# Attention in a two-block transformer: third and fourth maximum and the diagonal follow one another on VectorE; the products of a head's first maximum run one head ahead on TensorE

## The chip, the cores and the metric

The kernel runs on one core of one Trainium2 chip. The metric is the device time of an execution in microseconds (us); lower is better. The five engines of a core (TensorE or PE, VectorE or DVE, ScalarE or ACT, GpSimd or POOL, SyncE or SP) each work through their own queue in order and wait on each other through semaphores. "PEld" in the profile is TensorE's loading of weights, which overlaps its matmuls.

## What is computed

The reference is two transformer blocks on 512 tokens of width 1024. The part that matters here is the attention of the first block: 8 query heads over 2 key and value heads, 512 latent queries against 768 keys (256 of a context, 512 latent).

```python
def gqa_block(q, k, v):
    B, Q = q.shape[:2]
    qg = q.reshape(B, Q, ATTN_KV_HEADS, GQA_GROUP, HEAD_DIM)
    s = jnp.einsum('bqkgd,btkd->bkgqt', qg, k, preferred_element_type=jnp.float32) * ATTN_SCALE
    p = jax.nn.softmax(s, axis=-1).astype(v.dtype)
    o = jnp.einsum('bkgqt,btkd->bqkgd', p, v)
    return o.reshape(B, Q, ATTN_WIDTH)
```

The softmax subtracts each query's maximum over the 768 keys. After the attention the heads are multiplied by `w_out`. Beside it the kernel still has to compute 24 "modulation rows", dot products of a conditioning vector with 128 rows of `w_mod` each, which nothing needs before the attention is over.

## The kernel before

One program for each engine, written out by hand; what stands in the code is the order in which an engine runs. Products are made of rounded high parts and low remainders (`q_high`, `q_low`, `Kst`, `K2`), so a head's scores take two matmuls for each tile.

The attention is one loop over the 8 heads, with these steps for head h:

- **First pass, for the maxima (TensorE, L814 `row_max(h, qt)`, qt 0 to 3).** 128 queries on the partitions, 768 keys along the free dimension: two matmuls of 512 and two of 256 columns, into banks 0 and 1 (even qt) or 2 and 3 (odd qt). VectorE's `att_max(h, qt)` (L1958) reduces the 768 columns to one maximum for each query. A bank pair is free again once the maximum before the last was taken (`pe.wait_ge(a_mx, u - 1)`).
- **Diagonal and row (VectorE, then TensorE).** `att_diagonal(h)` spreads the four columns of maxima over four diagonal blocks `Dg`; `shift_row(h)` (matmul L839) multiplies them by ones, which gives the negative maxima as a row over the 512 queries in bank 4. ScalarE (`shift_high`, L1290) and VectorE (`shift_low`, L1978) write it into spare partitions of `q_low`, so that the second pass subtracts it.
- **Second pass (TensorE, `scores(h, kt)`, kt 0 to 5, L850 and L851).** 128 keys on the partitions, 512 queries along the free dimension, in banks 4 and 5 by turns. `scores(h, 0)` waits for `shift_low(h)`. ScalarE takes the exponential (`exponent`, L1298) into `PA` or `PB`, and `values(h, kt)` (L863) accumulates the product with the values, and the sum of the exponentials.
- **Scaling.** ScalarE's `inverse_sum(h)` (L1307, L1308), after the second exponential of the next head; VectorE's `att_scale(h)` (L1986) and, for each pair of heads, `att_low` (L1991).
- **Queries of the next pair.** VectorE's `query_low(t, e)` (L1949, L1950) in iterations 0, 2 and 4, once ScalarE's `query_high` is there.
- **Modulation rows.** VectorE's `modulation_row` (L1930) reads one 512 KB unit that SyncE has loaded into one of the four buffers `wraw`. Each row read lets SyncE load the next unit: unit k of this row series needs k - 3 rows read; behind the 24 units come the units of `w_out`, whose first needs 21 rows read, the second 22. Between them stands the load of `crow`.

Iteration h of the loop holds the second pass of head h and the first pass of head h + 1. ScalarE's order around the last head is fixed: before `exponent(7, 4)` stands the rounding of the first unit of `w_out` (`split_hi`, L580), which waits for that unit's load.

In the words of the rows below, "head h" stands for iteration h. Iterations 1, 3 and 5 are called odd, 2, 4 and 6 even.

## Time and profile before

| | |
|---|---|
| median of 3 runs | 1503.74 us (1501.14 to 1504.5) |
| the profiled execution | 1504.83 us, span 1503.0 us |
| TensorE busy | 1420.6 us, 95% of the span |
| VectorE busy | 913.9 us, 61% |
| ScalarE busy | 540.7 us, 36% |
| the chain that ended last | TensorE 86%, VectorE 9%, ScalarE 2% |
| the loop over heads | from 266.89 us (`scores(0, 0)`) to 366.27 us (first matmul of `w_out`) |

TensorE's busy share is that of the whole program; its matmuls are pipelined, so in a stretch where TensorE waits now and then, the waits have to be read from the rows. The profiled execution took 1.1 us more than the median of the runs.

### The profile page before, as it was taken

To read this page: it belongs to the slowest core of one execution; us is meant where nothing else is said; L and a number is where in the kernel's file an instruction comes from. 1 tells how busy PE (TensorE), PEld (TensorE's weight loads), DVE (VectorE), ACT (ScalarE), POOL (GpSimd) and SP (SyncE) were. 2 spreads that over 40 slices of the span, in tenths; PEclk is the share of its full clock that TensorE was granted. 3 is DMA by queue.
4 is the path that set the end of the run, shared out by engine and by line. 5 is a ranking of instruction groups with operands and counts; after the bars stand their busy time and mean duration, and the time that the engine had idled before them with its cause. 6 is when DMAs were issued, how large, how long until landed. Compare 5 with 4: busy or idle time off the path is not lost.

```text
span 1503.0 us, 16624 instructions
## 1 busy us (share of the span) xinstructions
PE 1420.6 (95%) x6132; PEld 1103.4 (73%) x6132; DVE 913.9 (61%) x1232; ACT 540.7 (36%) x754; POOL 102.7 (7%) x117
## 2 busy tenths in 40 slices
PE   6899999999969999999999999999879999999996
PEld 4688887555738888888884487767768888888885
DVE  5744487886166666663235674888537888886222
ACT  2523353544352323222222553332343433333221
POOL 0002530000300000000110020000020000000010
PEclk9799999999989999999999999999989999999999
DMA  9222230235216666664421022120112322323211
GB/s 371 81 77 84 78 107 21 85 112 182 84 50 245 209 223 223 213 235 143 152 81 43 28 85 70 57 100 26 56 70 85 98 98 87 108 89 126 100 62 56
DMA packets 44514, 169.19 MB, mean 113 GB/s; under 512 B 5516, under 2 KB 6092, under 8 KB 43181
## 3 DMA queue, kind: packets, MB, share of 16 engines
q1 hardware_dynamic: 43052, 165.60, 31.5%
q0 software_dynamic: 1408, 2.89, 0.7%
q8 instruction: 33, 0.54, 0.1%
q14 instruction: 21, 0.16, 0.0%
HBM read 163.49 MB, written 2.10 MB: 110 GB/s over the span
## 4 chain that ended last, share of the span: by engine, by line
PE 86%; DVE 9%; ACT 2%; issue 2%; DMA 1%; SPq 0%; POOL 0%; DVEq 0%; ACTq 0%
PE PS L597 71%; PE PS L966 4%; PE PS L654 2%; DVE tb L1698 2%; DVE sink L1930 1%; PE PS L1087 1%; DVE H L1698 1%; DVE dert L1958 1%; PE PS L617 1%; PE PS L642 1%; PE PS L863 1%; DMA wraw<-w_mod_a 1%; DVE wsp L586 1%; PE PS L839 1%; PE PS L725 1%
## 5 line engine op out<-in xcount | busy, mean ns | idle before, releaser
L597 PE MATMUL PS<-H,wsp 128*128 128x512 f32 x3600 | 843.5, 395 | 26.6 <-DVE H L1698 17.7
L597 PEld LDWEIGHTS PS<-H,wsp 128*128 128x128 f32 x3600 | 681.3, 190 | 183.9 <-issue 23.4
L586 DVE TENSOR_TENSOR wsp<-wraw,wsp 128x1024 fp32r<-128x1024 f32 (+1 forms) x182 | 237.3, 1304 | 439.5 <-ACT wsp L580 439.2
L580 ACT ACTIVATE wsp<-wraw 128x1024 fp32r<-128x1024 f32 (+1 forms) x182 | 202.6, 1114 | 523.7 <-PE PS L597 522.0
L597 PE MATMUL PS<-hid,wsp 128*128 128x512 f32 x1056 | 240.0, 389 | 0.0
L597 PEld LDWEIGHTS PS<-hid,wsp 128*128 128x128 f32 x1056 | 198.2, 188 | 41.8 <-issue 0.8
L1698 DVE SCALAR_TENSOR_TENSOR cva<-PS,dert,cva 128x441 f32<-128x441 f32 (+2 forms) x176 | 122.2, 695 | 5.5
L1930 DVE CUSTOM_DVE_ANT_0 sink<-mring,crow_t,colt 128x1024 bf16<-128x1024 f32 x56 | 71.7, 1280 | 0.4
L1621 POOL COPY acc<-sqb 128x512 f32<-128x512 f32 x4 | 4.4, 1093 | 809.9 <-ACT sqb L1413 287.5
L1624 POOL TENSOR_TENSOR acc<-acc,sqb 128x512 f32<-128x512 f32 x24 | 41.2, 1717 | 202.0 <-ACT sqb L1599 82.6
L654 PE MATMUL PS<-sqb,ones 128*128 128x512 f32 (+1 forms) x64 | 34.8, 696 | 8.9 <-ACT sqb L1126 8.8
L1397 ACT ACTIVATE hid<-hv 128x512 f32 (+1 forms) x22 | 13.9, 632 | 70.3 <-DVE hv L2113 70.3
L1698 DVE SCALAR_TENSOR_TENSOR ca<-cb__144,colt,ca 128x512 f32<-128x512 f32 x40 | 33.8, 845 | 3.2 <-ACT ca L1478 2.5
L654 PEld LDWEIGHTS PS<-sqb,ones 128*128 128x128 f32 x64 | 13.8, 244 | 28.4 <-issue 17.1
L1644 POOL DMA_DIRECT2D RS<-RU x44 | 21.8, 502 | 183.2 <-ACT RU L1221 146.8
L1579 ACT ACTIVATE sl<-cva,colt 128x512 f32<-128x512 f32 x22 | 15.9, 725 | 49.9 <-DVE cva L1698 49.9
L1126 ACT ACTIVATE sqb<-X 128x512 f32<-128x512 f32 x32 | 19.9, 627 | 38.4 <-PE PS L654 23.0
L1958 DVE TENSOR_REDUCE dert<-PS 128x1 f32<-128x768 f32 x32 | 30.4, 950 | 4.1 <-PE PS L829 3.9
L1930 DVE CUSTOM_DVE_ANT_0 sink<-wraw,crow_t,colt 128x1024 bf16<-128x1024 f32 x24 | 30.7, 1278 | 0.4
L1131 ACT ACTIVATE H<-tb,dert 128x512 fp32r<-128x512 f32 x32 | 22.3, 721 | 22.9 <-DVE tb L1698 22.9
L597 PEld LDWEIGHTS PS<-Hc,wsp 128*128 128x128 f32 x240 | 30.0, 192 | 0.7
L597 PE MATMUL PS<-Hc,wsp 128*128 128x256 f32 x240 | 30.2, 283 | 0.0
(277 smaller groups left out, 1295.0 us busy)
## 6 DMA issues: line engine op xcount, KB each, us to landing
mring<-mod_c SPq DMA_DIRECT2D x56, 512.0 KB, 4.5
wraw<-w_ffn_in SPq DMA_DIRECT2D x44, 512.0 KB, 3.3
wraw<-w_up SPq DMA_DIRECT2D x44, 512.0 KB, 3.2
wraw<-w_mod_b SPq DMA_DIRECT2D x24, 512.0 KB, 3.3
wraw<-w_hy_in SPq DMA_DIRECT2D x24, 512.0 KB, 3.2
wraw<-w_w_in SPq DMA_DIRECT2D x22, 512.0 KB, 3.2
wraw<-w_ffn_out SPq DMA_DIRECT2D x16, 704.0 KB, 4.1
wraw<-w_down SPq DMA_DIRECT2D x16, 704.0 KB, 4.0
```

The costliest lines, as they stand in the source:

```text
L580: nc.scalar.activation(wsp[:, o % 2, 0, 0:n], wraw[:, g % RAW, 0:n], ACT.Copy).then_inc(w_hi, 1)
L586: nc.vector.tensor_tensor(wsp[:, o % 2, 1, 0:n], wraw[:, g % RAW, 0:n], wsp[:, o % 2, 0, 0:n].bitcast(F32), ALU.subtract).then_inc(w_lo, 1)
L597: mm = nc.tensor.matmul(psum, wsp[:, o % 2, a, wk * P:(wk + 1) * P], h[:, b, kt, :], start=first and kt == kts[0] and (a, b) == (0, 0), st ...
L654: nc.tensor.matmul(PS[:, bank, 0:n], ones[:, :], sqb[:, q % 2, 0:n], start=kt == 0, stop=kt == KT - 1).then_inc(n_acc, 1)
L966: mm = nc.tensor.matmul(PS[:, b0 + a, :], fwdt[:, a, mt, f * P:(f + 1) * P], src[:, (a // 2) * 2 + mt, c * 512:(c + 1) * 512], start=mt == ...
L1126: SC.activation(sqb[:, q % 2, 0:n], src, ACT.Square).then_inc(n_sq, 1)
L1131: SC.activation(dst, tb[:, (k * KT + kt) % 4, 0:n], ACT.Identity, bias=shift).then_inc(n_hi, 1)
L1624: PL.tensor_tensor(acc_of(k), acc_of(k), sqb[:, q % 2, 0:n], ALU.add).then_inc(n_acc, 1)
L1644: ins = pool.dma_start(moved_tile(n)[to:to + HALF, :], RU[of:of + HALF, n % 2, 0:L])
L1698: return VE.scalar_tensor_tensor(out=o, in0=a, scalar=s, in1=b, op0=op0, op1=op1)
L1930: VE.tensor_tensor_reduce(sink[:, :], unit, crow_t[:, which, :], 1.0, bias, ALU.mult, ALU.add, to).then_inc(m_rd, 1)
L1958: VE.tensor_reduce(der("mx", u), PS[:, b:b + 2, :].rearrange("p a b -> p (a b)")[:, 0:LA], mybir.AxisListType.X, ALU.max).then_inc(a_mx, 1)
```

## The change

On TensorE `row_max(h + 1, 0)` leaves its place behind `scores(h, 0)` and is issued at the end of the iteration before, behind `values(h - 1, 5)`; that of head 1 stands ahead of the loop. On VectorE `att_max(h + 1, 0)` moves in the same way, behind `shift_low`. `att_max(h + 1, 2)`, `att_max(h + 1, 3)` and `att_diagonal(h + 1)` follow one another, where a modulation row or a half of `query_low` stood between the second and third, and another between the third and fourth maximum. The pieces taken out go behind the diagonal, behind the first maximum, and to the iteration's end. ScalarE's, GpSimd's and SyncE's orders stay as they are, and no instruction is added or dropped.

```diff
--- before.py
+++ after.py
@@ -883,10 +883,9 @@
                     inner_values(t)
             shift_row(0)
             gn_variance(3)
+            row_max(1, 0)
             for h in range(8):
                 scores(h, 0)
-                if h < 7:
-                    row_max(h + 1, 0)
                 scores(h, 1)
                 if h < 7:
                     row_max(h + 1, 1)
@@ -899,6 +898,8 @@
                     shift_row(h + 1)
                 values(h, 4)
                 values(h, 5)
+                if h < 6:
+                    row_max(h + 2, 0)
 
 
             pe.wait_ge(a_mx, 32)
@@ -2034,9 +2035,8 @@
             gn_low(1)
             shift_low(0)
             dve.wait_ge(crow_on, 1)
+            att_max(1, 0)
             for h in range(8):
-                if h < 7:
-                    att_max(h + 1, 0)
                 if h == 0:
                     gn_scale(2)
                     gn_gate(3)
@@ -2044,34 +2044,32 @@
                     att_scale(h - 1)
                 if h < 7:
                     att_max(h + 1, 1)
+                if h == 0:
+                    gn_scale(3)
+                    gn_low(2)
+                elif h < 7:
+                    modulation_row(next(mod_next))
+                if h < 7:
+                    att_max(h + 1, 2)
+                    att_max(h + 1, 3)
+                    att_diagonal(h + 1)
                 if h % 2 == 0 and h < 6:
                     query_low(h // 2 + 1, 0)
                 elif h < 7:
                     modulation_row(next(mod_next))
                 if h < 7:
-                    att_max(h + 1, 2)
-                if h == 0:
-                    gn_scale(3)
-                    gn_low(2)
-                elif h % 2 == 0 and h < 6:
+                    shift_low(h + 1)
+                if h < 6:
+                    att_max(h + 2, 0)
+                if h % 2 == 0 and h < 6:
                     query_low(h // 2 + 1, 1)
                 elif h < 7:
                     modulation_row(next(mod_next))
-                if h < 7:
-                    att_max(h + 1, 3)
-                    att_diagonal(h + 1)
                 if h == 0:
-                    query_low(1, 1)
+                    gn_low(3)
                 elif h % 2 == 0:
                     att_low(h // 2 - 1)
-                if h % 2 and h < 7:
-                    modulation_row(next(mod_next))
                 if h < 7:
-                    shift_low(h + 1)
-                    modulation_row(next(mod_next))
-                if h == 0:
-                    gn_low(3)
-                if h % 2 == 0 and h < 6:
                     modulation_row(next(mod_next))
             for m in mod_next:
                 modulation_row(m)
```

On TensorE, around the end of iteration 0 and the start of iteration 1 (L839 is the row of maxima, L863 the values, L828 and L829 the products for a maximum, L850 and L851 the scores), the order changes like this:

```order
 L863 MATMUL PS<-PA,V 128x512 x2
-L850 MATMUL PS<-H,Kst 128x512
-L851 MATMUL PS<-H,K_96 128x512
-L828 MATMUL PS<-Kst,QS_93 128x512
-L829 MATMUL PS<-K_96,QS_93 128x512
-L828 MATMUL PS<-Kst,QS_93 128x256
-L829 MATMUL PS<-K_96,QS_93 128x256
+L828 MATMUL PS<-Kst,QS_93 128x512
+L829 MATMUL PS<-K_96,QS_93 128x512
+L828 MATMUL PS<-Kst,QS_93 128x256
+L829 MATMUL PS<-K_96,QS_93 128x256
+L850 MATMUL PS<-H,Kst 128x512
```

Rows with "-" are the order of before, rows with "+" that of the change. The four products for the maximum now stand between the last values and the first scores.

On VectorE, before, from the shift of head 4 (iteration 3's end) to the diagonal of head 5 (iteration 4), where L1978 is `shift_low`, L1930 a modulation row with its accumulator read, L1958 a maximum, L1986 `att_scale`, L1949 and L1950 a half of `query_low`:

```order
267 L1978 TENSOR_TENSOR H<-PS,H 32x512
268 L1930 ISA sink,dert<-wraw,crow_t,colt 128x1024
270 L1958 TENSOR_REDUCE dert<-PS 128x1
271 L1986 TENSOR_TENSOR R<-PS,R 64x512
272 L1958 TENSOR_REDUCE dert<-PS 128x1
273 L1949 CAST QS_93<-QA 64x512
274 L1950 TENSOR_TENSOR QS_93<-QA,QS_93 64x512
275 L1958 TENSOR_REDUCE dert<-PS 128x1
276 L1949 CAST QS_93<-QA 64x512
277 L1950 TENSOR_TENSOR QS_93<-QA,QS_93 64x512
278 L1958 TENSOR_REDUCE dert<-PS 128x1
279 L1698 SCALAR_TENSOR_TENSOR Dg<-ident,dert 128x512
```

And the same stretch of the change (its lines have numbers one higher):

```order
259 L1979 TENSOR_TENSOR H<-PS,H 32x512
260 L1959 TENSOR_REDUCE dert<-PS 128x1
261 L1931 ISA sink,dert<-wraw,crow_t,colt 128x1024
263 L1931 ISA sink,dert<-wraw,crow_t,colt 128x1024
265 L1987 TENSOR_TENSOR R<-PS,R 64x512
266 L1959 TENSOR_REDUCE dert<-PS 128x1
267 L1931 ISA sink,dert<-wraw,crow_t,colt 128x1024
269 L1959 TENSOR_REDUCE dert<-PS 128x1 x2
270 L1699 SCALAR_TENSOR_TENSOR Dg<-ident,dert 128x512
```

The first maximum now stands right behind the shift, three modulation rows stand before the third maximum instead of one, and both halves of `query_low` have gone behind the diagonal. (The accumulator read behind each modulation row is left out of both listings.)

On VectorE, before, from the last diagonal to the first low part of `w_out` (L1991 is `att_low`, L586 the low part of a unit):

```order
310 L1698 SCALAR_TENSOR_TENSOR Dg<-ident,dert 128x512
311 L1991 TENSOR_TENSOR H<-R,H 128x512
312 L1978 TENSOR_TENSOR QS_93<-PS,QS_93 32x512
313 L1930 ISA sink,dert<-wraw,crow_t,colt 128x1024
315 L1986 TENSOR_TENSOR R<-PS,R 64x512
316 L1930 ISA sink,dert<-wraw,crow_t,colt 128x1024
318 L1930 ISA sink,dert<-wraw,crow_t,colt 128x1024
320 L1930 ISA sink,dert<-wraw,crow_t,colt 128x1024
322 L586 TENSOR_TENSOR wsp<-wraw,wsp 128x1024 x2
```

And the same stretch of the change:

```order
299 L1699 SCALAR_TENSOR_TENSOR Dg<-ident,dert 128x512
300 L1931 ISA sink,dert<-wraw,crow_t,colt 128x1024
302 L1979 TENSOR_TENSOR QS_93<-PS,QS_93 32x512
303 L1931 ISA sink,dert<-wraw,crow_t,colt 128x1024
305 L1992 TENSOR_TENSOR H<-R,H 128x512
306 L1931 ISA sink,dert<-wraw,crow_t,colt 128x1024
308 L1987 TENSOR_TENSOR R<-PS,R 64x512
309 L1931 ISA sink,dert<-wraw,crow_t,colt 128x1024
311 L1931 ISA sink,dert<-wraw,crow_t,colt 128x1024
313 L1931 ISA sink,dert<-wraw,crow_t,colt 128x1024
315 L586 TENSOR_TENSOR wsp<-wraw,wsp 128x1024 x2
```

Behind the last diagonal and ahead of `att_scale(6)` there were one modulation row and `att_low`; now there are three rows and `att_low`. The 21st row is in both orders the last one ahead of `att_scale(6)`.

## Rows read from the trace of the kernel before

**Rows 1.** Timeline of TensorE: start us, duration us, engine, line, tiles, idle before and releaser

```profile
276.79 1.13 PE L839 MATMUL PS<-Dg,ones 128*128 128x512 f32 x2 [0.65 <-DVE Dg L1698]
...
292.89 0.39 PE L828 MATMUL PS<-Kst,QS 128*128 128x512 f32 x1
...
302.77 1.12 PE L839 MATMUL PS<-Dg,ones 128*128 128x512 f32 x2 [1.20 <-DVE Dg L1698]
...
305.30 0.55 PE L850 MATMUL PS<-QS,Kst 128*128 128x512 f32 x1
...
315.67 1.12 PE L839 MATMUL PS<-Dg,ones 128*128 128x512 f32 x2 [1.04 <-DVE Dg L1698]
...
354.71 1.13 PE L839 MATMUL PS<-Dg,ones 128*128 128x512 f32 x2 [1.31 <-DVE Dg L1698]
```

**Rows 2.** Timeline of VectorE in an even iteration, head 2

```profile
293.78 0.96 DVE L1958 TENSOR_REDUCE dert<-PS 128x1 f32<-128x768 f32 x1 [0.22 <-PE PS L829]
...
299.88 0.42 DVE L1949 CAST H<-QA 64x512 fp32r<-64x512 f32 x1
...
301.03 0.96 DVE L1958 TENSOR_REDUCE dert<-PS 128x1 f32<-128x768 f32 x1
302.03 0.69 DVE L1698 SCALAR_TENSOR_TENSOR Dg<-ident,dert 128x512 f32<-128x512 f32 x1
...
304.56 0.68 DVE L1978 TENSOR_TENSOR QS<-PS,QS 32x512 fp32r<-32x512 f32 x1 [1.24 <-ACT QS L1290]
```

**Rows 3.** Timeline of VectorE in an odd iteration, head 3

```profile
305.27 1.28 DVE L1930 CUSTOM_DVE_ANT_0 sink<-wraw,crow_t,colt 128x1024 bf16<-128x1024 f32 x1
...
306.60 1.28 DVE L1930 CUSTOM_DVE_ANT_0 sink<-wraw,crow_t,colt 128x1024 bf16<-128x1024 f32 x1
...
309.20 0.68 DVE L1986 TENSOR_TENSOR R<-PS,R 64x512 f32<-64x512 f32 x1 [0.32 <-ACT R L1308]
309.81 0.94 DVE L1958 TENSOR_REDUCE dert<-PS 128x1 f32<-128x768 f32 x1
310.67 1.27 DVE L1930 CUSTOM_DVE_ANT_0 sink<-wraw,crow_t,colt 128x1024 bf16<-128x1024 f32 x1
...
311.87 0.94 DVE L1958 TENSOR_REDUCE dert<-PS 128x1 f32<-128x768 f32 x1
```

**Rows 4.** Timeline of VectorE in an even iteration, head 6

```profile
347.98 0.69 DVE L1986 TENSOR_TENSOR R<-PS,R 64x512 f32<-64x512 f32 x1 [1.41 <-ACT R L1308]
348.70 0.96 DVE L1958 TENSOR_REDUCE dert<-PS 128x1 f32<-128x768 f32 x1
349.69 1.29 DVE L1930 CUSTOM_DVE_ANT_0 sink<-wraw,crow_t,colt 128x1024 bf16<-128x1024 f32 x1
```

**Rows 5.** Timeline of all engines around head 7 and the start of `w_out`

```profile
358.53 9.68 SPq L466 DMA_DIRECT2D wraw<-w_w_out  x6
...
362.14 1.05 ACT L580 ACTIVATE wsp<-wraw 128x1024 fp32r<-128x1024 f32 x1
...
363.09 0.58 ACT L1298 ACTIVATE PB<-PS 128x512 f32<-128x512 f32 x1
...
364.10 1.98 PE L863 MATMUL PS<-PB,V 128*128 128x512 f32 x4
...
366.27 2.96 PE L597 MATMUL PS<-H,wsp 128*128 128x512 f32 x12 [0.20 <-DVE wsp L586]
```

**Rows 6.** DMA issues from 353.3 to 355 us, and from 358 to 359 us: KB each, us to landing

```profile
wraw<-w_mod_b SPq DMA_DIRECT2D x1, 512.0 KB, 3.4
...
wraw<-w_w_out SPq DMA_DIRECT2D x1, 512.0 KB, 3.4
```

**Rows 7.** Stretches of 1 us: busy us of PE, PEld, DVE, ACT, POOL, then PE clock, DMA share, GB/s

```profile
355.00:356.00 1.00, 1.00 (x3) 0.39 (x3) 0.26 (x1) 0.13 (x1) 0.00 (x0) 1.00 0.99 385
...
380.00:381.00 1.00, 1.00 (x4) 0.81 (x3) 1.00 (x1) 0.78 (x2) 0.62 (x1) 0.50 0.81 246
```

**Rows 8.** Timeline of TensorE ahead of the third unit of `w_out`

```profile
379.20 21.16 PE L597 MATMUL PS<-H,wsp 128*128 128x512 f32 x85 [1.81 <-DVE wsp L586]
```

## The prediction, made before the changed kernel ran

> **What bounds the kernel now.** I read the busy table first: TensorE works 95% of the span, so only its waits can be won back. Then TensorE's timeline through the loop over heads. Before every row of maxima (L839) TensorE stands still until VectorE's diagonal is done: 0.65 us in head 0, later 1.04, 1.20 and 1.31 us [rows 1]. From the first of these rows in the loop, at 276.79 us, to the last, at 354.71 us, there are six whole periods: 77.92 us, 12.99 us each [rows 1]. Within a period TensorE has about 11.8 us of work (302.77 to 315.67 us is 12.90 us, less the wait of 1.04 us [rows 1]). The most that the loop can give is therefore 6 x 1.2 = 7 us, 0.5% of the kernel.
>
> Then VectorE's timeline, since it is what TensorE waits for. I measure from start to start, because that is what adds up. VectorE reads its products in an order that makes it wait first for ScalarE (0.32 us ahead of `att_scale` in head 3 [rows 3], 1.41 us in head 6 [rows 4]) and then run without a pause to the diagonal. So the diagonal is late because of what stands between `att_scale` and it, and the change takes pieces out of just that stretch. The question is what VectorE waits for once they are gone.
>
> **The clockwork.** I put time 0 at the start of a row of maxima (L839) and call it T. Each fixed distance comes from one pair of rows:
>
> - the diagonal starts at T - 0.74 (302.03 against 302.77 us) [rows 1, 2];
> - `shift_low` starts at T + 1.79 (304.56 us) [rows 2], and the next head's first scores at T + 2.53 (305.30 us) [rows 1];
> - on VectorE, start to start: `att_scale` to maximum 0.61, maximum to modulation row 0.86, modulation row to maximum 1.20, modulation row to modulation row 1.33 (all [rows 3]); in even heads, where `att_scale` works on the other half of the partitions, `att_scale` to maximum 0.72 and maximum to modulation row 0.99 [rows 4]; half a `query_low` to the next instruction 1.15 (299.88 to 301.03 us), maximum to diagonal 1.00 [rows 2]. For maximum to maximum, of which the trace has no unwaited pair, I take 0.86 as to a modulation row; 1.00 would be its upper bound. For `att_low` I take 0.61, that of `att_scale`.
>
> **The change part by part.**
>
> *TensorE.* The four products of the first maximum move ahead of `scores(h + 1, 0)`. Their place is T + 2.53, but the values ahead of them still stream: the first scores took 0.55 instead of 0.39 us there [rows 1], so I add 0.16 and let them start at T + 2.69. VectorE took the maximum 0.89 us after such products began (292.89 to 293.78 us) [rows 1, 2]. So the first maximum starts at T + 3.58 and no sooner. TensorE's own work stays what it was. The wait for `shift_low`, which the values alone just covered, is now covered with 0.7 us to spare, and is worth nothing.
>
> *VectorE.* After `shift_low` (done at T + 2.5) stands the first maximum, and VectorE idles until T + 3.58. That is a new wait of about 1.1 us in each head, and behind it stands everything that leads to the next diagonal. From there, in an even head: maximum 0.99, two modulation rows 1.33 each, `att_scale` 0.72, maximum 0.99, modulation row 1.20, maximum 0.86, maximum to diagonal 1.00. The sum is 8.42, the diagonal stands at T + 12.00 and the next row of maxima at T + 12.74. In an odd head: maximum 0.99, half a `query_low` 1.15, `att_low` 0.61, modulation row 1.20, `att_scale` 0.61, maximum 0.86, modulation row 1.20, maximum 0.86, and 1.00 to the diagonal. That is 8.48, and T + 12.80. ScalarE's part of `att_scale` was there at T + 6.43 in head 3 (309.20 us) [rows 1, 3] and comes a little later now, about T + 6.6; VectorE gets to `att_scale` at about T + 7.2, so that old wait is gone. TensorE waits a little before the products of the fourth maximum, whose banks come free when the second is read, but finishes the last scores at about T + 12.6, still ahead of the row.
>
> Six periods, three of each kind, make 76.6 us against 77.9: **the loop gives 1.3 us**. Head 0 I cost at 0.1 us gained: there VectorE still stands before `gn_low(2)` until ScalarE has its copy ready behind the fourth exponential, which covers all that was pulled forward. If that cover were gone, head 0 would give at most its wait of 0.65 us [rows 1].
>
> *The tail.* Here a price stands that is easy to miss. Of the 24 modulation rows fewer are read early: one instead of two in head 0, four instead of three in head 6. The 21st row, which lets SyncE load the first unit of `w_out`, was read right behind the last `shift_low`; that load was issued at 358.53 us, T + 3.82 [rows 1, 5]. Now behind `shift_low` (T + 2.51) stand row 20, `att_low` and row 21: 1.20 + 0.61 later, so the load goes out at T + 5.65. Row 20 in turn releases the last unit of the modulation rows and the load of `crow`, at T + 3.85; before, they went out a good 5 us ahead of `w_out`. So three transfers of 512 KB are in flight together. Alone such a unit lands 3.4 us after its issue [rows 6], and at the full rate of 385 GB/s [rows 7] each further one needs 512 KB / 385 GB/s = 1.36 us. They land at T + 7.25, 8.6 and 9.95. Bounds for the first unit of `w_out`: T + 9.05 if nothing gets in its way, T + 9.95 if all queue up; I take the later one, since the rate in the row is that of full DMA engines (0.99 busy).
>
> Who waits for it: ScalarE's `split_hi`, and behind it on ScalarE `exponent(7, 4)` and `exponent(7, 5)`, and for them TensorE's last two value products and with them `w_out`. Before, ScalarE was free for it at 362.14 us (T + 7.43) and found it landed. It took 0.95 us to the next exponential, and TensorE went on at 364.10 us without a pause, T + 9.39 [rows 5]. Now: 9.95 + 0.95 + 0.65 for the exponential = T + 11.5. So TensorE idles about 2.1 us, and `w_out` starts 2.1 us later than it would, at T + 13.6 instead of T + 11.56 (366.27 us [rows 1, 5]). With the early landing it is 1.2 us. **The tail takes 2.1 us.** Nothing after that changes its order.
>
> *Sum.* -1.3 - 0.1 + 2.1 = +0.7 us. Against the profiled execution's own 1504.83 us this is 1505.5; its median of runs lies 1.1 us lower, which gives **1504.4 us**. A measurement of this kernel can hardly tell less than 0.2%, 3.0 us, from no change.
>
> *A rule against the trace.* In the rows a modulation row starts 0.86 us after a maximum that lasts 0.94 us [rows 3], so VectorE's instructions overlap a little when none waits for another. The Trainium skill (VectorE: DVE Perf Modes, "The DRAIN you can't avoid") says that the next instruction does not start until the pipeline has emptied, and that chaining without semaphores does not help. By the trace the stretch to the diagonal takes 8.4 to 8.5 us; by that rule it would take more, as in the third rival below.
>
> **The rivals.**
>
> 1. *The tail costs more: the clock falls.* TensorE waited 1.81 us before 379.20 us [rows 8], and from 380 us its granted clock was 0.50, which is 1.2 of its 2.4 GHz [rows 7]; by the stretches beside it that lasted some 3.3 us, which costs 1.7 us of work. Not each such wait does this: of nine waits of 1.3 to 2.5 us in the trace I found a fall after three. A wait of 2.1 us in the tail is of that kind. Time: 1504.4 + 1.7 = 1506.1 us.
> 2. *The tail costs less.* The first unit of `w_out` lands by T + 9.05, 0.9 us sooner: 1503.5 us. For it: of the 3.4 us that a lone unit takes only 1.36 are movement at full rate, and the two transfers ahead of it have been under way for 1.8 and 1.4 us when it starts.
> 3. *Slower, from VectorE.* With two maxima in a row on other banks, and with semaphores between most pieces, each instruction starts only when the one before has ended. With full lengths (maximum 0.99, modulation row 1.36, `att_scale` and `att_low` 0.72) the stretches become 8.8 and 9.3 us, the periods 13.1 and 13.6, and six of them 80.1 us: 2.2 us slower instead of 1.3 faster. Time: 1504.4 + 3.5 = 1507.9 us, slower. That is 0.065 us for each of some nine instructions in six periods; from about 0.045 us each it decides, since 2.4 us more than the forecast is where slower begins. Against it: the same pairs overlap in the trace of before.
> 4. *Faster: TensorE becomes the bound.* If the first maximum came with no wait and VectorE were ready early in each head, the periods would be TensorE's 11.8 us: 7.1 us less, with the tail still 2.1 us more. Time: 1503.74 - 5.0 = 1498.7 us. Against it: VectorE can't start the first maximum before T + 3.58 and has 8.4 us of work from there to the diagonal.
>
> **How the numbers follow.** Forecast 0.45, rival 1 0.22, rival 2 0.13, rival 3 0.11, rival 4 0.09. The forecast, rival 1 and rival 2 all lie within 3.0 us of 1503.74, together 0.80; slower is rival 3, 0.11; faster is rival 4, 0.09. The range leaves out rival 4 and most of rival 3. It reaches down below rival 2 by the scatter of the runs, to 1502.0 us, and up past rival 1 to 1506.9 us.
>
> **What the changed kernel's profile would show.** Rows of maxima in the loop 12.7 to 12.8 us apart, with TensorE's wait for the diagonal down to 0.1 to 0.4 us; a wait of VectorE of about 1 us for the product of each first maximum, and none for ScalarE ahead of `att_scale`; a short wait of TensorE for the second maximum; the first load of `w_out` 5.6 us after the last row of maxima, ScalarE's first `split_hi` of `w_out` waiting for a DMA, and TensorE standing still for 1 to 2 us ahead of its last values. I am wrong if that load is not waited for (then it is faster by 1.4 us), if the periods stay at 13 us, or if they fall under 12.3.

## The result and the profile after

| | before | changed |
|---|---|---|
| median, first comparison | 1502.99 us (1499.59 to 1504.85, 20 runs) | 1505.97 us (1503.13 to 1508.52, 20 runs) |
| ratio, first comparison | | 1.0026, 95% interval [1.0019, 1.0033] |
| median, second comparison (`e11_change_timed`) | 1502.73 us (15 runs) | 1505.19 us (11 runs) |
| ratio, second comparison | | 1.0015, 95% interval [1.0006, 1.0024] |
| profiled execution | 1504.83 us, span 1503.0 us | 1505.25 us, span 1503.5 us |

The change makes the kernel slower: by 3.9 us (2.9 to 5.0) in the first comparison and 2.3 us (0.9 to 3.6) in the second. The mean of the two is 3.1 us. The busy table has hardly moved (page of the changed kernel; busy us, share of the span, instructions):

```profile
span 1503.5 us, 16624 instructions
PE 1419.8 (94%) x6132; PEld 1100.9 (73%) x6132; DVE 914.9 (61%) x1232; ACT 540.1 (36%) x754; POOL 102.1 (7%) x117
```

So the difference lies in waits, and in the clock. The spans of two single executions don't show it, since the program ahead of the loop and behind it scatters: in the thirteen traces of this study head 0's row of maxima starts anywhere from 260.3 to 264.5 us, and from the third unit of `w_out` to the end it takes 1121 to 1124 us. The second scatter goes with TensorE's clock: in six of the traces (before, changed, `e1`, `e2`, `e3`, `e9`) the granted clock falls to 0.50 just behind the third unit's wait, and the rest takes 1123.6 to 1124.3 us; in the other seven it stays at 1.00 there, and the rest takes 1121.1 to 1122.6 us. Executions of the changed kernel lie in both groups. I therefore compare stretches between fixed points: the eight rows of maxima (L839), the last head's last values (L863 behind the wait), and the start of the third unit of `w_out`, which waits 1.81 us for VectorE in each of the traces that I compare below. Each row of such numbers is one execution; of the kernel before there is one trace only.

| us | before | changed | difference |
|---|---|---|---|
| head 0: first row of maxima to second | 12.44 | 12.29 | -0.15 |
| loop: second to eighth row, six periods | 77.92 | 76.62 | -1.30 |
| eighth row to the last values | 9.39 | 12.15 | +2.76 |
| last values to the third unit of `w_out` | 15.10 | 16.38 | +1.28 |
| together | 114.85 | 117.44 | +2.59 |

TensorE's timeline of the changed kernel has these points (start, duration, idle before and what ended it). They answer to [rows 1] and [rows 8]:

```profile
274.21 1.12 PE L839 MATMUL PS<-Dg,ones 128*128 128x512 f32 x2 [1.19 <-DVE Dg L1699]
...
283.35 0.50 PE L828 MATMUL PS<-Kst,QS 128*128 128x512 f32 x1 [0.64 <-DVE dert L1959]
...
287.01 1.12 PE L839 MATMUL PS<-Dg,ones 128*128 128x512 f32 x2
...
299.76 1.12 PE L839 MATMUL PS<-Dg,ones 128*128 128x512 f32 x2 [0.16 <-DVE Dg L1699]
...
350.83 1.13 PE L839 MATMUL PS<-Dg,ones 128*128 128x512 f32 x2 [0.17 <-DVE Dg L1699]
...
362.98 3.52 PE L863 MATMUL PS<-PB,V 128*128 128x512 f32 x4 [2.58 <-ACT PB L1299]
365.51 12.04 PE L597 MATMUL PS<-H,wsp 128*128 128x512 f32 x48
...
379.36 2.14 PE L597 MATMUL PS<-H,wsp 128*128 128x512 f32 x6 [1.81 <-DVE wsp L586]
```

From the second row on, the waits for the diagonal have shrunk from 1.04 to 1.31 us to nothing or 0.17 us (in head 0 the wait has grown, from 0.65 to 1.19 us), and a new one of 0.64 us has come up inside the first pass. But the period is only 0.22 us shorter. And between the last row of maxima and the last values there is now a wait of 2.58 us where there was none.

VectorE's timeline in iteration 1 shows why the loop gives so little:

```profile
276.00 0.68 DVE L1979 TENSOR_TENSOR H<-PS,H 32x512 fp32r<-32x512 f32 x1 [0.69 <-ACT H L1291]
277.79 0.96 DVE L1959 TENSOR_REDUCE dert<-PS 128x1 f32<-128x768 f32 x1 [1.11 <-PE PS L829]
...
281.75 0.68 DVE L1987 TENSOR_TENSOR R<-PS,R 64x512 f32<-64x512 f32 x1
...
284.42 1.81 DVE L1959 TENSOR_REDUCE dert<-PS 128x1 f32<-128x768 f32 x2
286.26 0.69 DVE L1699 SCALAR_TENSOR_TENSOR Dg<-ident,dert 128x512 f32<-128x512 f32 x1
```

The first maximum (277.79 us) waits 1.11 us for its product; the old wait ahead of `att_scale` (L1987) is gone; the third and fourth maximum are one group (x2) and take 1.81 us together; the diagonal follows at once. One wait has taken the place of the other.

The tail, in a timeline of SyncE and one of ScalarE (the first start of a group of SyncE is the issue of its first load):

```profile
355.04 0.42 SPq L526 DMA_DIRECT2D crow_t<-crow  x1
356.47 3.69 SPq L466 DMA_DIRECT2D wraw<-w_w_out  x3
...
361.39 1.06 ACT L580 ACTIVATE wsp<-wraw 128x1024 fp32r<-128x1024 f32 x1 [3.00 <-DMA wraw<-w_w_out]
362.35 1.07 ACT L1299 ACTIVATE PB<-PS 128x512 f32<-128x512 f32 x2
```

In [rows 5] the load of `w_out` went out 3.82 us after the last row of maxima, and ScalarE found it landed. Now it goes out after 5.64 us, is there 4.9 us later, and ScalarE has stood still for 3.00 us in front of `split_hi`, with the two exponentials (x2, 362.35 us) behind it that TensorE needs.

Then the clock. Stretches of 1 us (busy us of PE, PEld, DVE, ACT, POOL; then the granted clock of PE, the DMA share, GB/s):

```profile
358.00:359.00 1.00, 1.00 (x5) 0.66 (x4) 0.96 (x3) 0.38 (x1) 0.00 (x0) 1.00 1.14 401
359.00:360.00 1.00, 1.00 (x4) 0.48 (x3) 0.96 (x3) 0.00 (x0) 0.00 (x0) 1.00 0.82 324
360.00:361.00 1.00, 0.40 (x2) 0.00 (x0) 1.00 (x1) 0.00 (x0) 0.00 (x0) 1.00 0.88 205
361.00:362.00 1.00, 0.00 (x0) 0.00 (x0) 0.13 (x2) 0.61 (x1) 0.00 (x0) 1.00 0.82 328
...
364.00:365.00 1.00, 1.00 (x2) 0.41 (x2) 0.61 (x1) 0.36 (x1) 0.00 (x0) 0.50 0.99 377
365.00:366.00 1.00, 1.00 (x3) 0.34 (x1) 0.62 (x1) 0.00 (x0) 0.00 (x0) 0.50 0.99 193
```

TensorE did nothing from 360.4 to 363.0 us, and behind it the granted clock was 0.50 (1.2 of 2.4 GHz), back at 1.00 from 367 us on. In the kernel before it stood at 1.00 from 363 to 369 us.

### The profile page after: what moved, and what is told of

It is laid out like the page before. It is cut to its first block, busy times and chain, and to the rows that moved or that the text cites. A ratio compares the mean times of both kernels' runs of the same rounds, so it can differ in the third digit from the quotient of the medians.

```text
span 1503.5 us, 16624 instructions
## 1 busy us (share of the span) xinstructions
PE 1419.8 (94%) x6132; PEld 1100.9 (73%) x6132; DVE 914.9 (61%) x1232; ACT 540.1 (36%) x754; POOL 102.1 (7%) x117
## 4 chain that ended last, share of the span: by engine, by line
PE 86%; DVE 9%; issue 2%; ACT 2%; DMA 1%; SPq 0%; POOL 0%; DVEq 0%; ACTq 0%
PE PS L597 71%; PE PS L967 4%; PE PS L654 2%; DVE tb L1699 2%; DVE dert L1959 1%; PE PS L863 1%; DVE sink L1931 1%; PE PS L1088 1%; DVE H L1699 1%; PE PS L617 1%; PE PS L642 1%; DMA wraw<-w_mod_a 1%; DVE wsp L586 1%; PE PS L839 1%; PE PS L725 1%
## 5 line engine op out<-in xcount | busy, mean ns | idle before, releaser
L586 DVE TENSOR_TENSOR wsp<-wraw,wsp 128x1024 fp32r<-128x1024 f32 (+1 forms) x182 | 238.0, 1308 | 440.4 <-ACT wsp L580 439.9
```

The source lines that it names most:

```text
L586: nc.vector.tensor_tensor(wsp[:, o % 2, 1, 0:n], wraw[:, g % RAW, 0:n], wsp[:, o % 2, 0, 0:n].bitcast(F32), ALU.subtract).then_inc(w_lo, 1)
```

## The experiments

All times are device medians against the kernel before on the same chip. `e1` to `e4` share one set of runs of it (1501.91 us, 21 runs), `e5` to `e8` another (1502.68 us, 29 runs). The table has the stretches of the section above.

| us | head 0 | six periods | row 8 to last values | to third unit | together, against before | ratio |
|---|---|---|---|---|---|---|
| before | 12.44 | 77.92 | 9.39 | 15.10 | 0 | |
| changed | 12.29 | 76.62 | 12.15 | 16.38 | +2.59 | 1.0026, 1.0015 |
| `e1_row_early` | 12.30 | 76.59 | 10.05 | 14.70 | -1.21 | 0.9998 [0.9988, 1.0007] |
| `e2_row_late` | 12.47 | 77.82 | 12.64 | 14.68 | +2.76 | 1.0021 [1.0011, 1.0030] |
| `e3_wait_filled` | 12.28 | 71.04 | 9.87 | 14.69 | -6.97 | 0.9952 [0.9936, 0.9968] |
| `e4_maxima_together` | 12.98 | 71.62 | 9.96 | 14.72 | -5.57 | 0.9955 [0.9941, 0.9968] |
| `e5_crow_later` | 12.28 | 76.62 | 11.63 | 16.34 | +2.02 | 1.0000 [0.9987, 1.0014] |
| `e6_split_behind` | 12.29 | 76.63 | 25.92 to the third unit | | -0.01 | 0.9994 [0.9983, 1.0005] |
| `e7_first_ahead` | 11.76 | 80.50 | 24.54 to the third unit | | +1.95 | 1.0013 [1.0001, 1.0025] |
| `e8_best` | 10.94 | 70.94 | 24.14 to the third unit | | -8.83 | 0.9936 [0.9920, 0.9951] |
| `e9_change_again` | 12.29 | 76.62 | 12.14 | 16.37 | +2.57 | |
| `e10_change_third` | 12.28 | 76.61 | 11.90 | 16.33 | +2.27 | |
| `e11_change_timed` | 12.29 | 76.63 | 13.30 | 17.56 | +4.93 | 1.0015 [1.0006, 1.0024] |

My theory: the loop gains 1.3 us and no more, because VectorE waits for the product of the first maximum; the tail loses more than that, because the 21st modulation row is read one or two instructions later and the first unit of `w_out` with it; and the clock falls on top. The rivals: the loss comes from VectorE (its instructions back to back cost more than they did apart), or from the products moved ahead on TensorE, and the tail would have been hidden.

### The tail alone: `e1_row_early` and `e2_row_late`

`e1` is the change with one more modulation row read in head 0, where VectorE waits 2.4 us for ScalarE anyway. All later rows move up by one, so the load of `w_out` goes out where it did before.

```diff
                 if h == 0:
                     gn_scale(3)
+                    modulation_row(next(mod_next))
                     gn_low(2)
```

> The change, with one modulation row more in head 0, in VectorE's wait for ScalarE's copy (2.44 us ahead of gn_low(2) in the changed kernel's profile). The 21st row is then read one place earlier and the first load of w_out goes out about 1.8 us earlier, with the load of crow well ahead of it. Theory A (the loss is the late load of w_out's first unit, with the fall of TensorE's clock behind the wait for it; the loop itself gains 1.3 us): TensorE's wait of 2.6 us ahead of its last values is gone, the granted clock stays at 1.00 there, and the kernel is 1.0 to 1.5 us faster than before, ratio 0.999 to 0.9995; from the last row of maxima to w_out 11.5 us instead of 14.7. Theory B (the loss sits in the rearranged loop or behind it, and the late load only takes up slack): the wait goes but the time stays within 1 us of the changed kernel's, ratio about 1.002.

Rows of `e1`, timelines of SyncE, ScalarE and TensorE:

```profile
354.45 7.29 SPq L466 DMA_DIRECT2D wraw<-w_w_out  x5
...
359.07 1.06 ACT L580 ACTIVATE wsp<-wraw 128x1024 fp32r<-128x1024 f32 x1 [0.91 <-DMA wraw<-w_w_out]
...
360.67 1.98 PE L863 MATMUL PS<-PB,V 128*128 128x512 f32 x4 [0.48 <-ACT PB L1299]
```

`e2` is the other half: the kernel before, with its maxima and its products where they were, and one modulation row fewer in head 0 and one more in head 6, behind `att_low(2)`. The rows between come one place later too, and the 21st is read where the change reads it.

```diff
-                elif h % 2 == 0:
+                elif h % 2 == 0 and h < 6:
                     att_low(h // 2 - 1)
...
-                if h % 2 == 0 and h < 6:
+                if h == 6:
+                    att_low(2)
+                if h in (2, 4, 6):
                     modulation_row(next(mod_next))
```

> The kernel before, with its loop untouched but for the rows: one modulation row fewer in head 0, one more in head 6, and att_low(2) between the last two, so that the 21st row is read as late after the last row of maxima as in the change. Theory A: w_out's first load goes out at about T + 5.6 and lands 4.3 to 5 us later, TensorE waits 2 to 2.6 us ahead of its last values and its clock falls to 0.50 for about 3 us in some or all executions; from the last row of maxima to w_out 13.6 to 14.7 us, and the kernel is 2 to 4 us slower than before, ratio 1.0015 to 1.0027. Theory B: no more than 0.5 us slower.

Rows of `e2`, the same timelines:

```profile
357.26 5.01 SPq L466 DMA_DIRECT2D wraw<-w_w_out  x4
...
362.67 1.06 ACT L580 ACTIVATE wsp<-wraw 128x1024 fp32r<-128x1024 f32 x1 [3.52 <-DMA wraw<-w_w_out]
...
364.27 1.98 PE L863 MATMUL PS<-PB,V 128*128 128x512 f32 x4 [3.10 <-ACT PB L1298]
```

And the stretch of 1 us in which `w_out` starts, granted clock 1.00:

```profile
365.00:366.00 1.00, 1.00 (x4) 0.38 (x2) 0.32 (x1) 0.65 (x1) 0.00 (x0) 1.00 0.70 274
```

With the load at 3.83 us behind the row (354.45 against 350.62 us), TensorE's wait falls from 2.58 to 0.48 us, the clock stays at 1.00, and the loss is gone: 0.9998. With the load at 5.63 us (357.26 us) and the maxima untouched, the kernel is slower by 3.2 us (1.7 to 4.5), about as much as with the whole change. So the late row in the tail is what turns the change into a loss. In the trace of `e2` the clock did not fall, though TensorE stood still for 3.10 us.

### What the two moves are worth in the loop: `e3`, `e4`, `e7`

`e3` is `e1` with VectorE's wait filled: the piece that stands behind the first maximum goes ahead of it.

```diff
-                if h < 6:
-                    att_max(h + 2, 0)
                 if h % 2 == 0 and h < 6:
                     query_low(h // 2 + 1, 1)
                 elif h < 7:
                     modulation_row(next(mod_next))
+                if h < 6:
+                    att_max(h + 2, 0)
```

> e1 with the piece that stood behind the first maximum (a modulation row, in even heads the second half of query_low) put ahead of it, into VectorE's wait of 1.1 us for the product. Theory A (VectorE's chain from T + 3.58 to the diagonal sets the period, and the wait ahead of it is what the move of the first maximum costs): each period falls from 12.77 to 11.8 or 11.9 us, where TensorE's own work ends it, six of them gain 5 to 6 us over e1, and the kernel is 6 to 7 us faster than before, ratio 0.9955 to 0.996. Theory B (the period is already near what TensorE and ScalarE allow): under 2 us faster than e1.

`e4` keeps the third and fourth maximum and the diagonal together, with `e1`'s early row, but both engines take the first maximum where the kernel before did.

```diff
-            row_max(1, 0)
             for h in range(8):
                 scores(h, 0)
+                if h < 7:
+                    row_max(h + 1, 0)
...
-                if h < 6:
-                    row_max(h + 2, 0)
...
-            att_max(1, 0)
             for h in range(8):
+                if h < 7:
+                    att_max(h + 1, 0)
...
-                if h < 6:
-                    att_max(h + 2, 0)
```

> One part of the change alone: third and fourth maximum and the diagonal together on VectorE, the first maximum and its products back in their old places, the extra row in head 0 as in e1. Theory A (the new wait for the first maximum's product is what eats the gain of the new order): VectorE fills the stretch behind shift_low with rows, reaches the diagonal about 1 us earlier, periods of 11.7 to 12.0 us, the kernel 5 to 7 us faster than before, ratio 0.9955 to 0.9965. Theory B (running one head ahead is what lets the first maximum come early, without it the old waits return): periods of 12.8 us or more, ratio 0.999 to 1.001.

`e7` is the reverse: the first maximum one head ahead as in the change, its products on TensorE too (not in this cut), the rest of VectorE's order as in the kernel before.

```diff
             for h in range(8):
-                if h < 7:
-                    att_max(h + 1, 0)
...
                     shift_low(h + 1)
+                if h < 6:
+                    att_max(h + 2, 0)
+                if h < 7:
                     modulation_row(next(mod_next))
```

> The other part of the change alone: the products of the first maximum and the maximum itself one head ahead, everything else on VectorE in the order of before (the rows of the tail too, so that w_out's first load is as early as before). Theory A (VectorE's new wait for the product is pure loss as long as nothing is put into it): VectorE waits about 1.1 us behind shift_low in each head and nothing is taken out of the stretch to the diagonal; periods of 13.2 to 13.7 us, the kernel 1.5 to 4 us slower than before, ratio 1.001 to 1.003. Theory B (the move relieves TensorE ahead of the second pass, and so gives something of its own): periods under 12.9 us, ratio under 0.9995.

Timelines of VectorE and TensorE in `e3`:

```profile
301.94 0.96 DVE L1959 TENSOR_REDUCE dert<-PS 128x1 f32<-128x768 f32 x1
...
307.42 1.80 DVE L1959 TENSOR_REDUCE dert<-PS 128x1 f32<-128x768 f32 x2
309.25 0.69 DVE L1699 SCALAR_TENSOR_TENSOR Dg<-ident,dert 128x512 f32<-128x512 f32 x1
...
298.28 1.13 PE L839 MATMUL PS<-Dg,ones 128*128 128x512 f32 x2
...
310.00 1.13 PE L839 MATMUL PS<-Dg,ones 128*128 128x512 f32 x2
```

In `e4`:

```profile
301.37 1.13 PE L839 MATMUL PS<-Dg,ones 128*128 128x512 f32 x2
...
313.42 1.02 PE L839 MATMUL PS<-Dg,ones 128*128 128x512 f32 x2
```

In `e7`:

```profile
300.05 1.13 PE L839 MATMUL PS<-Dg,ones 128*128 128x512 f32 x2 [1.23 <-DVE Dg L1699]
...
303.63 0.96 DVE L1959 TENSOR_REDUCE dert<-PS 128x1 f32<-128x768 f32 x1 [1.11 <-PE PS L829]
...
313.62 1.12 PE L839 MATMUL PS<-Dg,ones 128*128 128x512 f32 x2 [1.26 <-DVE Dg L1699]
```

In `e3` the first maximum no longer waits (301.94 us, nothing in brackets), the rows of maxima don't wait for the diagonal either, and the period is 11.84 us, TensorE's own. In `e4` it is 11.94 us, nearly the same, without the first maximum moved at all. In `e7`, with the first maximum moved and the rest left apart, it is 13.42 us, longer than the 12.99 us of before. So keeping the maxima together is what pays (6.3 us in six periods of `e4`), and moving the first maximum ahead loses (2.6 us in `e7`), because VectorE idles 1.1 us for it in each head with all of the path to the diagonal behind it. The change does both, but the two do not simply add up: -6.3 and +2.6 would be -3.7 us, and the change has -1.3. With the maxima together the first maximum ahead costs 5.0 us (76.62 against 71.62 us in `e4`), with the maxima apart 2.6; no run takes that difference to pieces. It is the unfilled wait that costs, not the place: with the wait filled, the six periods of `e3` are 0.6 us shorter than those of `e4`, and its head 0 is 0.7 us shorter (12.28 against 12.98 us, with the same extra row). In head 0 the first maximum ahead helps in `e7` as well (11.76 us, 12.44 us before).

This also settles my third rival: two maxima in a row take 1.80 to 1.82 us (changed kernel, `e3`), so the second starts 0.86 us or so after the first, as I had assumed from the pairs of the trace before. `e3` and `e4` have the same instructions next to one another and are 0.5% faster than before.

### Inside the tail: `e5` and `e6`

`e5` is the change with the load of `crow` taken out of the way: behind the first four units of `w_out` instead of ahead of them.

```diff
-            sp.wait_ge(r_q, NPAIR)
-            sp.dma_start(crow_t[:, 1, :], crow[:, 1]).then_inc(s_crow, 16)
             for i in range(8):
                 load_static("w_out", i)
+                if i == 3:
+                    sp.wait_ge(r_q, NPAIR)
+                    sp.dma_start(crow_t[:, 1, :], crow[:, 1]).then_inc(s_crow, 16)
```

> The change with the load of crow put behind the first four loads of w_out on SyncE's queue, instead of ahead of them; nothing else. If the first unit of w_out lands late because it shares the DMA engines with the two transfers ahead of it (4.9 us in the changed kernel's profile, 3.4 us alone), it now has one transfer ahead of it and lands 3.5 to 4.2 us after its issue; TensorE's wait ahead of its last values shrinks from 2.6 to 1.6 to 2.0 us, and the kernel is 0.7 to 2 us faster than the change, ratio to before 1.001 to 1.002. If the lateness of the issue alone is the cause, landing and time stay as they are (ratio about 1.0025).

`e6` is the change with `split_hi` of the first unit of `w_out` moved on ScalarE behind `exponent(7, 5)`, so that the last exponentials don't stand behind a load.

```diff
-                if h == 7:
-                    split_hi(act, "w_out", 0)
                 exponent(h, 4)
...
                 else:
+                    split_hi(act, "w_out", 0)
                     split_hi(act, "w_out", 1)
```

> The change with ScalarE's split of w_out's first unit put behind the last two exponentials instead of ahead of them; the load is as late as in the change. If the loss comes through ScalarE's order (the exponentials stand behind an instruction that waits for a load), TensorE's values run on without the wait of 2.6 us, and what is left is a wait of about 1.5 us at the first matmul of w_out: from the last row of maxima to it 12.8 to 13.2 us instead of 14.7, kernel 1.5 to 2 us faster than the change, ratio 1.001 to 1.0015. If the late unit alone counts, whoever waits for it, w_out starts as late as in the change (ratio about 1.0025).

`e5`, timelines of SyncE, ScalarE and TensorE:

```profile
358.80 5.00 SPq L466 DMA_DIRECT2D wraw<-w_w_out  x4
363.85 0.43 SPq L529 DMA_DIRECT2D crow_t<-crow  x1
...
363.21 1.06 ACT L581 ACTIVATE wsp<-wraw 128x1024 fp32r<-128x1024 f32 x1 [2.50 <-DMA wraw<-w_w_out]
...
364.80 2.85 PE L864 MATMUL PS<-PB,V 128*128 128x512 f32 x4 [2.08 <-ACT PB L1300]
```

And its stretch of 1 us at the start of `w_out`, granted clock 0.50:

```profile
366.00:367.00 1.00, 1.00 (x3) 0.41 (x2) 0.71 (x1) 0.25 (x1) 0.00 (x0) 0.50 0.98 303
```

`e6`, ScalarE and TensorE:

```profile
363.92 1.06 ACT L580 ACTIVATE wsp<-wraw 128x1024 fp32r<-128x1024 f32 x1 [0.30 <-DMA wraw<-w_w_out]
...
366.38 11.16 PE L597 MATMUL PS<-H,wsp 128*128 128x512 f32 x48 [1.58 <-DVE wsp L586]
```

Without `crow` ahead of it the unit lands 4.4 us after its issue (358.80 to 363.21 us) instead of 4.9: it is 0.5 us less, and TensorE's wait falls from 2.58 to 2.08 us. But four executions of the changed kernel (below) have landings of 4.7 to 6.0 us, so 0.5 us between two single executions is not proof of what `crow` costs. The clock fell again in this trace. The ratio, 1.0000, is better than the +2.0 us of the trace; ten of its twelve runs lie under 1504 us and two at 1507.4. The two have the lowest granted clock in the mean of the execution, 0.974 against 0.976 to 0.980 in the ten, but where in the program it fell, or whether it stayed up in the tail, that mean does not tell. In `e6` `w_out` starts 12.94 us after the last row of maxima, against 14.68 us in the change and 11.56 us before; the wait is 1.58 us and the clock stays at 1.00. That is enough to bring the sum of the stretches back to that of before. Here the end of `w_out`'s first unit, not the exponentials, is what TensorE waits for, so a late load still costs something wherever it is waited for.

### Faster than both: `e8_best`

`e8` is `e3` with `e5`'s place for `crow`, and with `gn_low(2)`, ahead of which VectorE still waited 1.2 us for ScalarE in head 0, behind the diagonal.

```diff
                     modulation_row(next(mod_next))
-                    gn_low(2)
...
                     att_diagonal(h + 1)
+                if h == 0:
+                    gn_low(2)
```

> e3 (wait filled) with the load of crow behind the first four of w_out, and with gn_low(2) behind the diagonal of head 1 instead of ahead of the third maximum, where VectorE waited for ScalarE. Expected: the first period shorter by 0.8 to 1.2 us (TensorE's wait of 1.19 us there gone), w_out's first unit no longer waited for, 0.3 to 0.8 us; in all 1 to 2 us faster than e3, ratio to before 0.994 to 0.9948. If these places are covered by TensorE's own work, no difference to e3 (0.9952).

1491.89 us (1491.76 to 1494.31), 0.9936 [0.9920, 0.9951]: 9.6 us faster than the kernel before. Head 0 takes 10.94 us, 1.3 less than in `e3`; the six periods take 70.94 us, 0.1 less; and from the last row of maxima to the third unit it is 24.14 us, 0.4 less, with no wait of TensorE ahead of the last values. The interval of five runs is too wide to tell the ratio from that of `e3`.

### The same kernel three times more: `e9`, `e10`, `e11`

The first two are one execution each; they ask whether the fall of the clock comes each time. The third asks whether the 3.9 us of the first comparison hold more than the 2.6 us of its trace.

> The changed kernel itself, one more execution with a profile, to see what repeats. If the tail's cost is the late unit, then TensorE's wait ahead of its last values is again 2 to 3 us; if the fall of the clock behind it is a matter of chance, from the start of the last values to the third unit of w_out it is either 14.7 us (no fall) or about 16.4 us (a fall), and one of these two executions may show no fall.

> The changed kernel a third time with a profile; the same expectation as for the second. If executions of this kernel differ by several us (1503.1 to 1508.5 were seen), the stretches from the first row of maxima to the third unit of w_out differ only by the landing of w_out's first unit and by falls of the clock, and the loop's periods are the same 12.77 us.

> The changed kernel as it is, timed again in five rounds beside the kernel before. Its trace accounts for 2.6 us more than before from the first row of maxima to the third unit of w_out; the first comparison gave 3.9 us (2.9 to 5.0). If the trace holds all of the loss and the rest of the first comparison was the scatter of executions, the ratio is about 1.0017 and its interval takes in 1.0017. If something that the stretches do not show costs 1.3 us more, it is 1.0026 again. In the profiled execution: periods of 12.8 us, last values 12.1 us after the last row of maxima, granted clock 0.50 for some 3 us right behind them.

They took 1505.63, 1502.69 and 1503.64 us (the last is the profiled one of `e11`; its median stands above). Head 0 and the loop are the same to 0.02 us in all. The tail is not. `e11`, timelines of SyncE, ScalarE and TensorE:

```profile
353.38 1.43 SPq L526 DMA_DIRECT2D crow_t<-crow  x1
354.86 4.94 SPq L466 DMA_DIRECT2D wraw<-w_w_out  x4
...
360.89 1.06 ACT L580 ACTIVATE wsp<-wraw 128x1024 fp32r<-128x1024 f32 x1 [4.17 <-DMA wraw<-w_w_out]
...
362.48 3.78 PE L863 MATMUL PS<-PB,V 128*128 128x512 f32 x4 [3.76 <-ACT PB L1299]
```

And one stretch of 1 us behind the wait:

```profile
363.00:364.00 1.00, 1.00 (x2) 0.33 (x1) 0.31 (x2) 0.86 (x1) 0.00 (x0) 0.50 0.64 258
```

Here the load was issued at the same distance (5.68 us) and landed after 6.0 us instead of 4.9, TensorE waited 3.76 us, and the clock was at 0.50 to 368 us. The tail cost 2.3 us more than in the first trace of the same kernel. In four traces of the changed kernel the first unit of `w_out` landed after 4.9, 4.9, 4.7 and 6.0 us, the clock fell behind the wait or, in `e11`, within it, in all four, and the stretches together are longer than before by 2.59, 2.57, 2.27 and 4.93 us, 3.1 us in the mean. The mean of the two comparisons is 3.1 us too, but that agreement proves little: the intervals are over 2 us wide, all four are set against one trace of before, and `e11`'s execution, with the dearest tail, was among the faster ones of its kernel (1503.64 us, median 1505.19), since from the third unit to the end it took 1121.9 us where the first trace took 1124.1. I expected 1.0017 if the first trace held all of the loss, and 1.0015 came out: the second comparison needs no more than that trace holds. The first one does.

## Why the prediction was right and wrong

I forecast 1504.4 us, 0.7 us more than before, and no measurable difference. It came out at 1505.97 us and slower, 3.9 us by the ratio. The time lies in the range, in part by luck: I counted from 1503.74 us, the median of three runs, and the median of twenty is 1502.99. The upper end of the range was 3.2 us above my base, and the measured 3.9 us is more. The sign had a chance of 0.11, and that for another mechanism. I also said that under 3.0 us nothing could be told from no change; with twenty runs of each the interval is 2.1 us wide (2.9 to 5.0).

**Right, term by term.** The first maximum starts 3.58 us after the row of maxima (277.79 against 274.21 us), as worked out. The periods are 12.80 us in odd and 12.75 us in even heads, against 12.80 and 12.74. The loop gives 1.30 us, as said, and head 0 gives 0.15 us instead of 0.1. The waits moved as said: none for `att_scale`, 1.11 us for the first maximum, 0.64 us for the second on TensorE. The load of `w_out` went out at 5.64 us (5.65 said), and the split waited for it. Adding up pairs of starts from the trace worked here to a few hundredths.

**The step that failed is the landing of `w_out`'s first unit**, "T + 9.95 if all queue up", which I took as the upper bound of that load. It landed at 10.56 us in the first trace (361.39 against 350.83 us) and at 11.71 us in `e11`. I counted the three transfers issued up to it. The two ahead of it landed at 7.5 and 8.8 us, only 0.3 and 0.2 later than I had them; the third is where the sum broke.

Two explanations fit, both estimates, and no run separates them. One is that loads issued later take a share: rows 22 and 23 are read 2.0 and 3.4 us behind row 21, and so SyncE's group at 356.47 us holds three units of `w_out`, not one. From 355 us to the landing the DMA moved 1.8 MB by the stretches' GB/s, where the three transfers that I counted are 1.57 MB; 0.25 MB at 385 GB/s are 0.65 us, the size of the miss. In `e11` the same count from 354 us is 2.0 MB. The other is that the rate was not 385 GB/s: from 356 us to the landing it was 326 in the mean (205 to 401), and 1.57 MB take 0.7 us longer at that.

The late landing put the last values 0.65 us behind what I had said (12.15 against 11.5 us), but from there to the third unit it takes 14.70 us without a fall of the clock (`e1`; 14.68 in `e2`) against 15.10 before, which gave 0.4 us back. So without the clock the term of the tail is 2.4 us in the first trace (12.15 and 14.70 against 24.49 before), where I had 2.1.

**The larger miss is the clock, which I had as rival 1 with 0.22.** It fell in all four traces of the changed kernel. From the last values to the third unit of `w_out` it takes 16.3 to 16.4 us with the fall in the changed kernel, `e9`, `e10` and `e5`, and 14.7 us in `e1` to `e4` without it: the price is 1.7 us, as I had it, and 2.9 us in `e11` (17.56 us), where the clock was low for some 6 us. What failed was the chance. I counted three falls behind nine waits of 1.3 to 2.5 us anywhere in the program and took that as the chance for a wait in this place. In the five traces of this order of the last head with such a wait (the four and `e5`) it fell five times. Yet `e2`, with another order in the loop and the same tail, waited longer and kept its clock, so what decides it is open.

**The sum:** -1.30 - 0.15 + 2.36 + 1.68 = +2.59 us in the first trace, against my +0.7. Of the 1.9 us between, 1.7 are the clock and 0.3 the landing, less 0.05 in head 0. The comparison gave 3.9 us. The cause of the rest, 1.3 us (0.3 to 2.4), is not shown. `e11` has an execution with 2.3 us more in the same stretches, so part of it may be tails dearer than that of the first trace; part may lie outside the stretches, where single executions differ by more than that. With rival 1 I had 2.4 us more than before, just under what I had called measurable. Even with every mechanism named, each price was taken at its kind end, and so slower got too small a chance.

**The rule against the trace.** The Trainium skill (VectorE: DVE Perf Modes, "The DRAIN you can't avoid") would have each instruction start only when the one before has left the pipeline. The same section adds that an instruction that is not held back starts earlier, which I left out. The trace agrees with the addition and not with the rule as I used it: maximum to maximum takes 0.86 us with a length of 0.94 to 0.96 us, and my third rival, which stood on full lengths, is refuted by periods of 12.75 and 12.80 us where it wanted 13.1 and 13.6.

**What stays open.** Which of TensorE's waits are followed by a fall. And why the same load lands after 4.7 us in one execution and 6.0 us in another, though in `e11` `crow` and `w_out` were issued 4.20 and 5.68 us behind the row of maxima, against 4.21 and 5.64 us in the first trace. One thing goes with it: SyncE took 0.42 us to issue `crow` in the first trace, `e9` and `e10` (landings 4.9, 4.9, 4.7 us), 0.93 us in `e2` (5.4 us) and 1.43 us in `e11` (6.0 us). Which is the cause of which, or whether both come from a third thing, no run shows.

## What to carry to other kernels

Taking work out from between two instructions of a path helps only as far as the engine isn't then made to wait elsewhere on that path: a consumer pulled 1.1 us ahead of its producer ate most of the gain here, and one independent piece moved into that wait brought 5.8 us (`e3` against `e1`). When work is reordered that also releases buffers, follow each release to the load it starts and to who waits for that load, with all transfers that are issued before it lands: one read 1.8 us later cost more than six shorter periods gave. And where TensorE is left waiting in front of its next long stretch, give a fall of its clock a large chance, and look at more than one trace of the same kernel before naming its price.

## What was not expected of the hardware

- A fall of the granted clock to 0.50 does not follow from the length of TensorE's wait alone. In the tail it came behind waits of 2.08 us (`e5`), 2.35, 2.58, 2.59 us (changed kernel) and within one of 3.76 us (`e11`), and not behind 3.10 us (`e2`) or 1.58 us (`e6`). In the kernel before it came behind a wait of 1.38 us at 844 us and not behind one of 2.41 us at 978 us. Behind the same wait of 1.81 us, ahead of the third unit of `w_out`, it came in six of the thirteen traces; in `e9` and not in `e10`, two executions of the same kernel. The stretches of `e9` and then of `e10`:

```profile
381.00:382.00 1.00, 1.00 (x4) 0.81 (x3) 0.41 (x1) 0.13 (x1) 1.00 (x1) 0.50 0.99 410
```

```profile
381.00:382.00 1.00, 1.00 (x6) 0.79 (x6) 0.65 (x1) 0.37 (x1) 1.00 (x1) 1.00 0.93 332
```

- In `e11` the clock fell while TensorE was still waiting (0.78 from 361 to 362 us, with the values starting at 362.48 us), and was then low for some 6 us instead of 3.
- A 512 KB unit that lands in 3.4 us alone [rows 6] took from 4.4 to 6.0 us with other loads in flight, and varied by 1.3 us between executions of one kernel.
